# Latent attention in a two-block network: the reciprocal roots of the norms as one GpSimd power

## The reference, cut to what matters

```python
def _rms_norm(x, g):
    x32 = _f32(x)
    y = x32 * lax.rsqrt(jnp.mean(x32 * x32, axis=-1, keepdims=True) + EPS)
    return (y * _f32(g)).astype(x.dtype)

q = (_rms_norm(a_q, q_a_norm) @ w_uq).reshape(B, L, MLA_HEADS, QK_HEAD_DIM)
q = _rms_norm(q, q_norm)                # one root for each token and head
...
ckv = _rms_norm(a_kv[..., :KV_LORA_RANK], kv_a_norm)      # one root for each token
kv = (ckv @ w_ukv).reshape(B, L, MLA_HEADS, QK_NOPE_DIM + V_HEAD_DIM)
...                                     # the keys, each head with the shared rotary part,
                                        # go through _rms_norm(k, k_norm) too
```

## Time and profile before

| | |
|---|---|
| median of three runs | 3386.78 us (3382.04 to 3387.57) |
| the profiled execution | 3385.58 us |
| its span in the profile | 3383.8 us |
| mean granted TensorE clock | 0.983 |
| instructions | 40304 |
| latent attention, from its first root to its last product | 1027 to 1316 us of the span |

### The profile page before, as it was taken

The page is one execution under the profiler, slowest core; times in us unless marked ns, Lnnn a source line. Parts: engine busy times, 40 slices in busy tenths (PEclk is TensorE's granted clock), DMA queues, the critical chain, the costliest instruction groups (busy, mean ns, idle before and its releaser), DMA issues.

```text
span 3383.8 us, 40304 instructions
## 1 busy us (share of the span) xinstructions
PE 3242.3 (96%) x16296; PEld 2577.7 (76%) x16296; DVE 1434.3 (42%) x2558; ACT 1306.7 (39%) x2311; POOL 1401.2 (41%) x788
## 2 busy tenths in 40 slices
PE   7999999999988999999999999999999989999998
PEld 4865788888875556788886688888887778878886
DVE  5567332222246873321223766242222658433132
ACT  4222331212244665432333534353333543444243
POOL 2224432222343445444462146634455225554445
PEclk9999999999998999999999999999999999999999
DMA  6145223122122001323232020333333111122321
GB/s 250 55 153 193 75 101 115 46 71 61 57 79 85 13 13 44 126 78 117 77 121 87 26 74 10 126 108 89 105 86 121 51 44 54 50 90 79 115 78 60
DMA packets 85638, 286.08 MB, mean 85 GB/s; under 512 B 9771, under 2 KB 10347, under 8 KB 84940
## 3 DMA queue, kind: packets, MB, share of 16 engines
q1 hardware_dynamic: 85452, 283.50, 25.8%
HBM read 281.37 MB, written 2.10 MB: 84 GB/s over the span
## 4 chain that ended last, share of the span: by engine, by line
PE 85%; DVE 10%; ACT 2%; issue 1%; POOL 1%; DMA 1%; SPq 0%; DVEq 0%; ACTq 0%
PE ps L476 21%; PE ps L479 20%; PE ps L477 20%; PE ps L516 2%; PE ps L517 2%; PE ps L518 2%; PE ps L2016 2%; PE ps L2086 1%; PE ps L454 1%; PE ps L2435 1%; PE ps L2421 1%; PE ps L455 1%; PE ps L456 1%; PE ps L2917 1%; PE ps L1243 1%
## 5 line engine op out<-in xcount | busy, mean ns | idle before, releaser
L428 POOL TENSOR_TENSOR WL<-ring,WH 128x1024 fp32r<-128x1024 f32 (+2 forms) x443 | 962.4, 2176 | 1520.8 <-ACT WH L419 1520.4
L476 PE MATMUL ps<-HX,WH 128*128 128x512 f32 x1768 | 695.1, 393 | 3.0 <-POOL WL L428 3.0
L479 PE MATMUL ps<-HX,WL 128*128 128x512 f32 x1768 | 691.9, 391 | 0.0
L477 PE MATMUL ps<-HX,WH 128*128 128x512 f32 x1768 | 690.2, 390 | 0.0
L419 ACT CAST WH<-ring 128x1024 fp32r<-128x1024 f32 (+2 forms) x443 | 420.2, 950 | 371.0 <-PE ps L479 312.9
L476 PE MATMUL ps<-FR,WH 128*128 128x512 f32 x1120 | 418.8, 374 | 0.3 <-DVE FR L3011 0.2
L477 PE MATMUL ps<-FR,WH 128*128 128x512 f32 x1120 | 409.5, 373 | 0.0
L476 PEld LDWEIGHTS ps<-HX,WH 128*128 128x128 f32 x1768 | 332.4, 188 | 82.5 <-issue 7.4
L479 PE MATMUL ps<-FR,WL 128*128 128x512 f32 x1120 | 389.2, 373 | 0.0
L479 PEld LDWEIGHTS ps<-HX,WL 128*128 128x128 f32 x1768 | 333.7, 189 | 50.1
L477 PEld LDWEIGHTS ps<-HX,WH 128*128 128x128 f32 x1768 | 332.7, 188 | 48.9
(11 more groups left out here) (391 smaller groups left out, 5105.2 us busy)
## 6 DMA issues: line engine op xcount, KB each, us to landing
ring<-in_w_mod SPq DMA_DIRECT2D x96, 512.0 KB, 5.8
ring<-in_ffn_w_up SPq DMA_DIRECT2D x88, 512.0 KB, 3.4
ring<-in_w_up SPq DMA_DIRECT2D x88, 512.0 KB, 3.4
ring<-in_w_in_tok SPq DMA_DIRECT2D x40, 512.0 KB, 3.6
ring<-in_w_in_feat SPq DMA_DIRECT2D x32, 512.0 KB, 3.3
ring<-in_ffn_w_down SPq DMA_DIRECT2D x32, 384.0 KB, 3.1
ring<-in_w_out SPq DMA_DIRECT2D x32, 384.0 KB, 3.2
ring<-in_w_down SPq DMA_DIRECT2D x32, 384.0 KB, 3.1
```

What stands on the lines that cost most here:

```text
L428: pool.tensor_tensor(WL[:, p % SPLITS, 0:n], ring.ap(r), WH[:, p % SPLITS, 0:n], ALU.subtract).then_inc(*ring.frees(r, split.g, "low", p))
L476: pe.matmul(o, high, xh, first, False)
L477: pe.matmul(o, high, xl, False, False)
L479: m = pe.matmul(PS[bs[i]][:, 0:N], low, get(k)[0], False, last)
```

## The change

Each root is now one GpSimd TENSOR_TENSOR with the operation power, `x` to the power of a column `half` that holds -0.5. It is done for `rkv` at the end of `low_rank_g`, for the queries in step 3 of `heads_g` and for the keys in step 8. The factor 96 of the queries' root goes into the numbers under the root. VectorE keeps the negative `nrq`, which moves behind `rope_v`. New waits: GpSimd for the means, VectorE for the roots (`factors`, `keys`), ScalarE for `rkv` and for `factors`; and `mean_v` waits until GpSimd has read the numbers of the group before.

```diff
+        half = sb("half", [128, 1])
-            dve.tensor_scalar(epsq, ps("stat")[:, 0:4], EPS / 256, EPS * EPS, ALU.mult, ALU.add).then_inc(
-                *bank.emptied(("stat",), mla.v))
-            inverse_root_v(dve, mla, rkv, mkv, scratch24[:, 0:6], 1.0)
-            mla.v.mark("small")
+            dve.tensor_scalar(epsq, ps("stat")[:, 0:4], 96 * EPS / 256, 96 * EPS * EPS, ALU.mult, ALU.add).then_inc(
+                *bank.emptied(("stat",), mla.v, "small"))
...
             rest_to(pool, g.last + 3)
+            pool.wait_ge(*st0.g.at("half"))
+            pool.wait_ge(*mla.v.at("small"))
+            inverse_root_g(pool, rkv, mkv).then_inc(*mla.g.up("small"))
+
+        def inverse_root_g(pool, y, x):
+            return pool.tensor_tensor(y, x, half[:, 0:1].to_broadcast(list(x.shape)), ALU.pow)
...
-            act.wait_ge(*mla.v.at("small"))
+            act.wait_ge(*mla.g.at("small"))
...
                 if step in (1, 2, 5, 6, 7):
                     square_g(pool, n, step - 1 if step < 3 else step - 3)
+                elif step == 3:
+                    if n >= 2:
+                        pool.wait_ge(*att.a.at("exp", 16 * n - 17, 0))
+                        pool.wait_ge(*mla.v.at("factors", n - 2))
+                    pool.wait_ge(*mla.v.at("mean", n, 1))
+                    inverse_root_g(pool, rq[:, n % 2, :], meanq).then_inc(*mla.g.up("factors", n))
+                elif step == 8:
+                    if n:
+                        pool.wait_ge(*mla.v.at("heads", n - 1))
+                    pool.wait_ge(*mla.v.at("mean", n, 4))
+                    inverse_root_g(pool, fk, st2).then_inc(*mla.g.up("keys", n))
...
+                dve.wait_ge(*(mla.g.at("factors", n - 1) if x < 2 else mla.g.at("keys", n - 1)))
...
-            inverse_root_v(dve, mla, rq[:, g, :], meanq, nrq[:, g, :], 96.0)
-            dve.tensor_scalar(nrq[:, g, :], rq[:, g, :], -1.0, None, ALU.mult).then_inc(*mla.v.up())
-
-        def key_factors_v(dve, n):
-            inverse_root_v(dve, mla, fk, st2, scratch24, 1.0)
+            dve.wait_ge(*mla.g.at("factors", n))
+            dve.tensor_scalar(nrq[:, g, :], rq[:, g, :], -1.0, None, ALU.mult).then_inc(*mla.v.up("factors", n))

         def key_v(dve, n, x):
+            dve.wait_ge(*mla.g.at("keys", n))
...
             query_v(dve, n, 1)
-            query_factors_v(dve, n)
             yield
             rope_v(dve, qtok.rearrange("p t (h c) -> p t h c", h=4), 4, 64)
             mla.v.mark("queries", n)
+            query_factors_v(dve, n)
...
             mean_v(dve, n, 4)
-            key_factors_v(dve, n)
...
         def lat_exp_a(act, i):
+            act.wait_ge(*mla.g.at("factors", i // 16))
...
+            pool.memset(half[:, :], -0.5).then_inc(*st0.g.up("half"))
```

More of the change, by code:

```diff
@@ L1670, in program @@
         st2, meanq = sm[:, 160:184], sm[:, 256:272]
-        fk, scratch24 = sm[:, 272:296], sm[:, 296:320]
+        fk = sm[:, 272:296]
         SCALE = 96 ** -0.5
@@ L1933, in mean_v @@
             e = epsq[:, 2 * x:2 * x + 2] if x < 2 else epsk[:, 2 * x - 4:2 * x - 2]
-            dve.scalar_tensor_tensor(by_tile, by_tile, 1.0 / 96, e.unsqueeze(2).to_broadcast([128, 2, 4]), ALU.mult,
+            dve.scalar_tensor_tensor(by_tile, by_tile, 1.0 if x < 2 else 1.0 / 96, e.unsqueeze(2).to_broadcast([128, 2, 4]), ALU.mult,
                                      ALU.add).then_inc(*mla.v.up("mean", n, x))
@@ L1944, in query_factors_v @@
             if n >= 2:
-                dve.wait_ge(*att.a.at("exp", 16 * n - 17, 0))
                 dve.wait_ge(*att.v.at("max", 16 * n - 17))
-            inverse_root_v(dve, mla, rq[:, g, :], meanq, nrq[:, g, :], 96.0)
-            dve.tensor_scalar(nrq[:, g, :], rq[:, g, :], -1.0, None, ALU.mult).then_inc(*mla.v.up())
-        def key_factors_v(dve, n):
-            inverse_root_v(dve, mla, fk, st2, scratch24, 1.0)
+            dve.wait_ge(*mla.g.at("factors", n))
+            dve.tensor_scalar(nrq[:, g, :], rq[:, g, :], -1.0, None, ALU.mult).then_inc(*mla.v.up("factors", n))
         def key_v(dve, n, x):
             f, t = fk[:, 8 * x - 16:8 * x - 8], 2 * x - 4
+            dve.wait_ge(*mla.g.at("keys", n))
             dve.tensor_tensor(batch(x), batch(x), f.unsqueeze(2).to_broadcast([128, 8, 64]), ALU.mult).then_inc(*mla.v.up())
```

## The result

The changed kernel takes 3390.15 us, median of 20 runs (3385.99 to 3394.55), the kernel before 3386.55 us in 20 runs beside it. The ratio is 1.0013, with a 95% interval of 1.0007 to 1.0019: slower by 3.6 us, within the 0.2% that the prediction called no change, where 12 us less were forecast. The profiled execution is one of the longer ones, 3393.67 us (span 3391.8); the 20 runs are not one heap, six lie at 3386.0 to 3386.7 and six at 3393.7 to 3394.6 us.

What follows compares the result with a forecast made beforehand. VectorE's program was taken to bound some 25 of a group's 67 us in latent attention. Gains of 10.2 us (groups 1 to 3) and 1.2 (group 0) gave 3374.2 us, named as 3374.5; 8-in-10 range 3368 to 3390.

Steps and rivals of the forecast that it cites:

- the size of the power: GpSimd power taken as some twenty-five passes: 1.2 us for the keys' 24 columns, 0.9 for the queries' 16.
- The upper bound: Costliest cost allowed for a GpSimd power, 2.42 us from a 128x1024 row; total gain then 4.2 us, 3381.4 us.
- The first rival: GpSimd power is no vector routine: 0.21 us a column, 5.0 us for 24; 10.1 us loss, 3395.7 us; chance 0.17.
- The rival's line 23.4 - 6.7p: Total gain over groups 0 to 3 if the 24-column power takes p us; no gain at p = 3.5.
- The block by the power: GpSimd powers hold VectorE's two-operand instructions: 0.26 us per keys' power in groups 1 to 3; 1.64 us new blocking, group 0.
- comes 0.5 us later and finds the root there: After the keys' power, VectorE's key product `key_v` would not have to wait for the root.
- the 1.9 us gain there: Keys' root, groups 1 to 3: 2.17 us off VectorE's chain, less 0.26 us waiting for the power.
- The queries' root: Groups 1 to 3: 3.24 us leave VectorE, but the next maximum waits for TensorE; 1.50 us gained per group.
- Met waits: Added waits in `mean_v`, `lat_exp_a` and for old numbers concern things done tens of us before; no cost counted.
- the sum: Whole latent attention: 10.2 us from groups 1 to 3 plus 1.2 from group 0, 11.4 us gained; chance 0.58.
- The third rival: TensorE's second scores come earlier, so the queries' 3.24 us come off whole: 16 us gained, 3369.6 us; chance 0.10.
- The rival on TensorE's limit: TensorE, busy 28.15 of 32 us, takes half of each group's gain: 6.3 us left, 3379.3 us; chance 0.15.

Runs made afterwards that it cites:

- e7_unused_power: Changed kernel with keys' root back on VectorE and ScalarE's wait for the queries' root moved earlier, plus an unread 24-column GpSimd power: 3378.24 us, ratio 0.9977.
- e1_keys_v: Changed kernel with the keys' root back on VectorE as ten instructions: 3379.92 us, ratio 0.9982 to the kernel before.
- e9_short_power: Changed kernel with powers cut to 2 of 16 and 3 of 24 columns, a product writing the rest, output invalid: 3370.32 us, ratio 0.9955.
- e10_thirds: Changed kernel with ScalarE's wait moved earlier and the keys' power in three parts of 8 columns: 3370.40 us, ratio 0.9955.

## Why the prediction was wrong, point by point

- **The step that failed is the size of the power.** The prediction took "some twenty-five passes over its columns", 1.2 us for 24 columns, "nearer the lower one as the operands are 16 and 24 columns only". It is 4.16 us. At 0.161 us a column it is a hundred passes at 1.6 ns. The upper bound, 2.42 us from the costliest GpSimd row, was none either: it is a row of cheap work on many columns, and says nothing of dear work on few. The first rival, 0.21 us a column and 5.0 us, was the nearest of all the cases, and had 0.17.
- **What a power of that length does was partly foreseen.** The rival's line 23.4 - 6.7p gives -4.5 us at p = 4.16; measured are -3.6 in the medians and -6.7 in the stretches. The agreement is by luck: it rests on a block that isn't there, and lacks the late table load.
- **The block by the power does not exist.** The prediction charged 0.26 us for each keys' power and 1.64 us of new blocking in group 0. In `e7_unused_power` a power of 4.15 us holds no VectorE instruction. A long GpSimd product does, as before. The rule of the Trainium skill (SBUF — State Buffer, section Who interferes with whom: held for the whole instruction) is true in these traces of the scalings and not of this operation. By the prediction's own terms this put 3 x 0.26 us and, of the 1.64, the power's 0.9 on the wrong side, 1.7 us in all; the squares' part of the 1.64 is GpSimd products, and no run tries it.
- **What replaced it is latency.** The prediction said that `key_v` "comes 0.5 us later and finds the root there". It waits 2.81 us, then 1.3 us more behind the scaling that was queued after the power. Against `e1_keys_v` that is a loss of 3.2 to 3.4 us a group, instead of the 1.9 us gain there. How much of it is TensorE's lower clock depends on the execution: the clock falls behind the 2.45 us gap of the kernel before too, and 0.60 against 0.79 is worth 1.5 us.
- **The queries' root was right**: VectorE early, TensorE the floor at the next second part. In the changed kernel that part leaves TensorE at 1154.84, and the maximum waits for it and begins 0.63 us later, as forecast:

```profile
1154.84 0.60 PE L2029 MATMUL ps<-AR 96*128 96x256 f32 x2
...
1155.47 0.42 DVE L2039 TENSOR_REDUCE sm<-ps 128x1 f32<-128x256 f32 x1 [0.33 <-PE ps L2029]
```

Forecast were 1.50 us a group, measured 2.7, 1.5 and 1.5; the 1.2 us more in group 1 stay unexplained. The power's 3.5 us of latency are covered, as was said.
- **Met waits were costed at nothing.** As time on an engine they are nothing. But the one in `lat_exp_a` moved a table load that is in no source line, shown in the kernel before by one line: 3 us in the traces, but 0.1 to 1.9 us in the medians, which is not clear of the scatter.
- **With the power at its forecast length** the gain is 16.0 us in the medians and 13.4 in the stretches (`e9_short_power`), where the sum said 11.4. Groups 2 and 3 gave 3.9 us each against 3.41. Group 0 gave 3.1 against 1.2, which is within its scatter. Group 1 gave 2.4 us with the late load's 3.0 in it, so some 2 us more than forecast; the queries' root has 1.2 of them. The third rival said that less idle could lift the clock: behind the keys' root it is 1.00 in all groups here, while the code of the kernel before had 1.00, 0.79 and 0.60 there in its traces. That may be where the medians' further gain comes from; no run shows it.
- **The rival on TensorE's limit** (28.15 of 32 us busy) did not decide: `e10_thirds` takes 4.1 us out of group 2.

## What to carry to other kernels

An operation that no row shows has no upper bound in the dearest row of another operation: time it by itself first, or let its cost range over a hundred elementwise passes. When work moves to another engine, ask who waits for it and what is queued behind it there: here the power of the queries, whose user comes later, gained 5.7 us in three groups, and that of the keys, whose user comes at once, cost 10 us; cut into parts that follow their inputs, the keys' power turned that loss into a gain. Before a microsecond in a trace is put down to a change, look at what the same code does in a second trace: the granted clock alone moved a group by 1.5 us. Look for a table load behind every wait that is added ahead of an activation.

## What the hardware showed that was not expected

- A GpSimd power of 24 columns does not hold VectorE's two-operand instructions in its 4.15 us, while a product of 768 columns holds them for all of its 1.47 us. Why was not tried.
- TensorE's clock fell to its lower level, 1.2 GHz, behind gaps of 2.1 to 2.8 us in the changed kernel: granted 0.50 in one window of 6 us and 0.66 in one of 5. In the first, two groups of matmuls took 1.90 and 2.30 us, which at full clock take 1.01 and 1.23, so a gap can cost TensorE almost as much again as it lasts. Whether it does varies between executions: behind a gap of 2.45 us in the same code the clock over the next 8 us was 1.00, 0.79 or 0.60.
